# Delta rule: two sums of squares taken from rounded high and low parts, with the order tables set anew

## What is computed

```
q = l2_norm(q) * 128 ** -0.5 ; k = l2_norm(k)      # x * rsqrt(sum(x*x) + eps), sum over 128
kk = k k^T ; lower = strict(beta * kk * decay) ; sol = (I + lower)^-1 [v*beta, k*beta*exp(g)]
for each chunk:  v_new = u - w S ; o = q_dec S + qk v_new ; S = S*g_last + k_dec^T v_new
o = rms_norm(o, o_gain) * silu(z)                  # sum of o*o over 256
x = x + o @ w_out
```

## Time and profile before

| what | us |
|---|---|
| median of 3 runs | 1572.76 |
| the runs | 1573.16, 1568.33, 1572.76 |
| the profiled execution | 1573.43 |
| its span in the trace | 1571.5 |
| PE busy | 1538.3 (98%) |
| DVE busy | 897.3 (57%) |
| ACT busy | 751.1 (48%) |
| POOL busy | 258.9 (16%) |

### The profile page before, as it was taken

One profiled execution on the slowest core, in us unless ns is written; L12 is line 12 of the kernel. 1 busy time (PEld: TensorE's weight loads), 2 busy tenths in 40 slices (PEclk: granted clock), 3 DMA queues, 4 the chain that ended last, 5 costly groups with the idle time before them and its releaser, 6 DMA issues.

```text
span 1571.5 us, 20651 instructions
## 1 busy us (share of the span) xinstructions
PE 1538.3 (98%) x7640; PEld 1225.8 (78%) x7640; DVE 897.3 (57%) x1681; ACT 751.1 (48%) x1310; POOL 258.9 (16%) x453
## 2 busy tenths in 40 slices
PE   8989999999999999999999999999999999999998
PEld 6868888888888777777777787666678888888877
DVE  5667777776656366656667434555375243434476
ACT  4354455534543256666567323665555242322343
POOL 1033323433323003334333100000000000000000
PEclk9999999999989999999999999999999999999999
DMA  5221121111114232222222222121123322232221
GB/s 196 86 71 50 57 66 55 54 56 59 48 54 140 94 103 85 72 84 81 68 81 75 81 94 75 54 67 68 54 82 99 101 94 97 91 108 94 94 94 54
DMA packets 40163, 127.22 MB, mean 81 GB/s; under 512 B 4576, under 2 KB 9104, under 8 KB 40064
## 3 DMA queue, kind: packets, MB, share of 16 engines
q1 hardware_dynamic: 38112, 121.65, 24.0%
q0 software_dynamic: 1040, 3.27, 0.6%
q10 hardware_dynamic: 912, 0.99, 0.2%
HBM read 122.69 MB, written 2.15 MB: 79 GB/s over the span
## 4 chain that ended last, share of the span: by engine, by line
PE 87%; DVE 6%; ACT 3%; POOL 2%; issue 1%; DMA 0%; POOLq 0%; SPq 0%; ACTq 0%; DVEq 0%
PE ps L832 85%; PE ps L1194 2%; DVE wl L1941 1%; DVE qkv L1979 1%; PE ps L974 1%; ACT wh L1338 1%; ACT L L1747 1%; POOL L L2755 1%; DVE h L2589 1%; DVE mo L2583 1%; POOL uc L2725 1%; POOL masks L2723 0%; DVE L L2446 0%; DVE up L2076 0%; DVE cin L1993 0%
## 5 line engine op out<-in xcount | busy, mean ns | idle before, releaser
L832 PE MATMUL ps<-xr,wh 128*128 128x512 f32 x2752 | 882.8, 402 | 3.2 <-DVE xr L2382 1.2
L832 PEld LDWEIGHTS ps<-xr,wh 128*128 128x128 f32 x2752 | 507.0, 189 | 130.3 <-issue 31.0
L832 PE MATMUL ps<-xr,wl 128*128 128x512 f32 x1376 | 539.4, 392 | 0.0
L1941 DVE TENSOR_TENSOR wl<-wraw,wh 128x1024 fp32r<-128x1024 f32 x214 | 263.7, 1239 | 139.0 <-ACT wh L1338 137.4
L832 PEld LDWEIGHTS ps<-xr,wl 128*128 128x128 f32 x1376 | 259.4, 189 | 56.5
L1338 ACT ACTIVATE wh<-wraw 128x1024 fp32r<-128x1024 f32 x214 | 222.2, 1049 | 81.8 <-PE ps L832 79.9
L832 PE MATMUL ps<-xm,wh 128*128 128x512 f32 x640 | 198.8, 392 | 5.1 <-DVE xm L2576 2.7
L832 PEld LDWEIGHTS ps<-xm,wh 128*128 128x128 f32 x640 | 119.5, 188 | 33.6 <-DVE xm L2576 4.0
L2755 POOL TENSOR_SCALAR L<-L,m 128x256 f32<-128x256 f32 (+1 forms) x128 | 99.4, 796 | 272.0 <-DVE m L2461 272.0
L832 PE MATMUL ps<-xm,wl 128*128 128x512 f32 x320 | 124.6, 389 | 0.0
L1979 DVE SCALAR_TENSOR_TENSOR qkv<-cin,gains,qkv 128x512 f32<-128x512 f32 x96 | 81.8, 853 | 10.6 <-ACT qkv L1368 9.7
(11 more groups left out here) (265 smaller groups left out, 1754.6 us busy)
## 6 DMA issues: line engine op xcount, KB each, us to landing
wraw<-in_wa SPq DMA_DIRECT2D x48, 512.0 KB, 3.7
wraw<-in_wb SPq DMA_DIRECT2D x32, 512.0 KB, 4.2
wraw<-in_wu SPq DMA_DIRECT2D x32, 512.0 KB, 3.6
wraw<-in_wd SPq DMA_DIRECT2D x32, 512.0 KB, 3.7
wraw<-in_wao SPq DMA_DIRECT2D x16, 512.0 KB, 3.7
wraw<-in_wbo SPq DMA_DIRECT2D x16, 512.0 KB, 3.9
wraw<-in_wc SPq DMA_DIRECT2D x16, 512.0 KB, 3.7
bias<-rel_rows SPq DMA_DIRECT2D x16, 256.0 KB, 3.9
```

The costliest lines, as they stand in the source:

```text
L832: return e.matmul(out, w, x, start=start, stop=stop, skip_group_check=True)
L1941: e.tensor_tensor(m.wl[:, i % N_SPLIT, :], m.raw[:, i % N_RAW, :], m.wh[:, i % N_SPLIT, :].bitcast(F), ALU.subtract).then_inc(s.wlo, 1)
```

## The change

ACT makes a rounded copy of k's squares in `rqr[1]` (a new step "khi" in p1), DVE the rounded difference in `rqr[0]` ("klo", in p2), and PE sums both with a rounded matrix of ones, two fp32r products in place of one fp32 product. On PE the sum moves from p1 to p2 and waits for klo. For the output's squares DVE makes both parts (a copy and a difference, in r9), and PE's r10 waits for the second. The rounded ones are written by ACT once, in head 0's p1. The tables `a1`, `a2`, `a8`, `a9` and `a` are replaced.

```diff
-    "a1": plan("p1 p2 p2 p0 p2 p1 p1 p0 p1 p16 p14 p20 p10 p30"),
-    "a2": plan("p1 p4 p2 q0 p2 q4 q1 q2 q0 p0 q2 p0 q2 p0 q3 r0 p1 r0 r1 p0 r0 r2 r1 p0 r2 r0 r0 p4 r2 p0 p2 p0 r6"),
-    "a8": plan("p0 q1 p2 q3 q1 q0 p0 q0 p3 q0 p0 q0 p0 q0 p1 r1 r0 r1 r0 p0 r0 p2 p0 r0 p0 r0 p2 r5 p0 r1 p0 r2 r1"),
-    "a9": plan("q1 q5 q2 q5 q3 q1 q3 q2 r9 r1 r3 r0 r1 r0 r2 r0 r4 r2 r4"),
-    "a": plan("p0 q2 q0 p4 q2 q0 p1 p1 q4 q0 p0 q1 p0 q1 p0 r2 r2 r0 p1 r0 p3 p1 r0 p2 r0 r1 r2 r3 p1 r2 p0 p2 r16"),
+    "a1": plan("p5 p3 p1 p1 p0 p0 p0 p0 p4 p19 p16 p14 p34 p4"),
+    "a2": plan("p5 q2 p0 q2 q2 q0 p1 q0 p1 q0 p0 q1 p0 q0 p3 r1 p1 r0 p0 p3 p2 r1 p4 p5 r0 r1 r0 r0 r1 p0 r6 r3 r0"),
+    "a8": plan("q5 q2 p0 p0 q1 q1 p0 q0 p1 q2 q0 p0 q1 r0 p0 r0 p0 r1 p0 r0 p0 r0 r0 r1 p1 p2 r0 p3 p1 r0 p0 r0 r1"),
+    "a9": plan("q2 q6 q2 q7 q1 q2 q1 q4 r5 r2 r1 r0 r2 r0 r1 r2 r4 r2 r3"),
+    "a": plan("p1 q4 q3 p3 q2 q0 p0 q1 q0 p1 q0 p1 q0 p0 r2 p0 r6 p1 r2 r0 r0 p0 r2 r1 p0 p0 r0 p1 p4 r1 p4 r7 r5"),
...
+        yield
         cleared(PREP_BANK)
-        e.wait_ge(s.prep_a, prep_a(h, "sqk"))
-        end(mm(m.banks[PREP_BANK][:], m.ones, m.rq[:, 0, :]), (s.prep_a, prep_a(h, "lnk")))
-        yield
+        e.wait_ge(s.prep_v, prep_v(h, "klo"))
+        mm(m.banks[PREP_BANK][:], m.onesr[:], m.rqr[:, 1, :], True, False)
+        end(mm(m.banks[PREP_BANK][:], m.onesr[:], m.rqr[:, 0, :], False, True), (s.prep_a, prep_a(h, "lnk")))
         yield
...
-        e.wait_ge(s.rec_v, REC_V * h + 5)
-        mm(m.banks[5][:], m.ones, m.sqh[:, 0, :]).then_inc(s.rec_p, 1)
+        e.wait_ge(s.rec_v, REC_V * h + 7)
+        mm(m.banks[5][:], m.onesr[:], m.sqhr[:, 1, :], True, False)
+        mm(m.banks[5][:], m.onesr[:], m.sqhr[:, 0, :], False, True).then_inc(s.rec_p, 1)
...
+        else:
+            e.wait_ge(s.unit, 3)
+            e.activation(m.onesr[:], m.ones, ACT.Copy)
         did(e.activation(m.rq[:, 0, :], m.qkv[:, par, 1, :], ACT.Square))
+        after("sqk")
+        if h:
+            e.wait_ge(s.prep_v, prep_v(h - 1, "qdn"))
+        did(e.activation(m.rqr[:, 1, :], m.rq[:, 0, :], ACT.Copy))
...
-        yield from idle(3)
+        yield from idle(1)
+        e.wait_ge(s.prep_a, prep_a(h, "khi"))
+        did(e.tensor_tensor(m.rqr[:, 0, :], m.rq[:, 0, :], m.rqr[:, 1, :].bitcast(F), ALU.subtract))
+        yield from idle(2)
...
+        e.wait_ge(s.rec_v, REC_V * h + 5)
+        did(e.tensor_copy(m.sqhr[:, 1, :], m.sqh[:, 0, :]))
+        e.wait_ge(s.rec_v, REC_V * h + 6)
+        did(e.tensor_tensor(m.sqhr[:, 0, :], m.sqh[:, 0, :], m.sqhr[:, 1, :].bitcast(F), ALU.subtract))
```

More of the change, by code:

```diff
@@ L521, in __init__ @@
         self.k1 = top.new([6 * 128 + N_CC + 64], name="k1")
+        moff = top.p
         self.masks = top.new([7, 128], name="masks")
+        self.onesr = at(moff + 512, [128], R, "ones")
         self.gains = top.new([N_GAIN + 128], name="gains")
@@ L549, in __init__ @@
         self.nb = a.new([15, 64], name="nb")
+        soff = a.p
         self.sqh = a.new([2, 512], name="sqh")
+        roff = a.p
         self.rq = a.new([2, 512], name="rq")
+        self.sqhr, self.rqr = at(soff, [2, 512], R, "sqhr"), at(roff, [2, 512], R, "rqr")
         self.qd = a.new([2, 512], name="qd")
@@ L746 @@
 PREP_A = {n: i + 1 for i, n in enumerate(
-    ("silu1", "sqk", "silu0", "silu2", "silu3", "lnk", "exk", "eb", "E", "sqq", "v0", "v1"))}
-PREP_V = {n: i + 1 for i, n in enumerate(("dv", "y", "at", "qk", "kg", "kd", "dc", "qdn", "U3", "T3"))}
+    ("silu1", "sqk", "khi", "silu0", "silu2", "silu3", "lnk", "exk", "eb", "E", "sqq", "v0", "v1"))}
+PREP_V = {n: i + 1 for i, n in enumerate(("klo", "dv", "y", "at", "qk", "kg", "kd", "dc", "qdn", "U3", "T3"))}
 PREP_O = {n: i + 1 for i, n in enumerate(("sel", "D"))}
@@ L754 @@
 LEV_O = {n: i + 1 for i, n in enumerate(("M4", "M5", "M6"))}
-REC_P, REC_A, REC_V = 12, 8, 9
+REC_P, REC_A, REC_V = 12, 8, 11
 STICK_P = {n: i + 1 for i, n in enumerate(
@@ L1089, in recur @@
         for j in range(2):
-            clear[6 + j] = [(s.rec_a, REC_A * h + 5 + j), (s.rec_v, REC_V * h + 6 + j)]
+            clear[6 + j] = [(s.rec_a, REC_A * h + 5 + j), (s.rec_v, REC_V * h + 8 + j)]
         yield
         cleared(5)
-        e.wait_ge(s.rec_v, REC_V * h + 5)
-        mm(m.banks[5][:], m.ones, m.sqh[:, 0, :]).then_inc(s.rec_p, 1)
+        e.wait_ge(s.rec_v, REC_V * h + 7)
+        mm(m.banks[5][:], m.onesr[:], m.sqhr[:, 1, :], True, False)
+        mm(m.banks[5][:], m.onesr[:], m.sqhr[:, 0, :], False, True).then_inc(s.rec_p, 1)
         clear[5] = [(s.rec_a, REC_A * h + 7)]
@@ L1608, in split_o @@
             e.wait_ge(s.wused, BLOCK["wa", 6 * HEADS - 1] + 1)
-        e.wait_ge(s.rec_v, REC_V * (i // 2) + 8 + i % 2)
+        e.wait_ge(s.rec_v, REC_V * (i // 2) + 10 + i % 2)
         e.activation(m.XR[:, i, :], m.XF[:, 16 + i, :], ACT.Copy).then_inc(s.ohi, 1)
@@ L2336, in recur @@
             e.wait_ge(s.rec_a, REC_A * h + 8)
-            e.wait_ge(s.rec_v, REC_V * h + 6 + j)
+            e.wait_ge(s.rec_v, REC_V * h + 8 + j)
             did(e.tensor_tensor(o, o, m.sqh[:, 0, :], ALU.mult))
```

## The result

| what | before | after |
|---|---|---|
| median, us | 1571.15 (4 runs) | 1578.54 (4 runs) |
| the profiled execution | 1573.43 | 1578.58 |
| its span | 1571.5 | 1576.5 |

The ratio is 1.0046, with a 95% interval of 1.0034 to 1.0059: slower, by 7.4 us in the medians and 5.0 us in the two spans. The forecast was 1573.3 and "no change". The time lies inside the range, on the side that I had given 0.24.

The account below looks back on a forecast made before the run. PE was taken as the bound, busy for 1538.3 of 1571.5 us. The terms -6.6 + 0.3 + 5.1 + 1.0 + 1.9 - 1.7 + 0.5 gave +0.5 us, so 1573.3 against the median 1572.76; range 1565.5 to 1579.5.

Parts of the forecast that it names:

- The price of a sum: On PE, two fp32r products take 0.45 us against 0.86; each sum saves 0.41 us, sixteen save 6.6 us.
- D: Rival: the sums save nothing, an fp32r pair taking as long as one fp32 product; +7.1 us, 1579.9, chance 0.02.
- P4 of head 0: At the start, P4 of head 0 starts 2.35 us later, at 117.0, with some 7 us idle before it.
- P4(0) to stage 3: Behind the start: 2.7 us of work left for later, and +1.0 us for the low clock behind P4 of head 0.
- The work left undone: Before P4 of head 0, fewer triples and no ks and G of head 1 are issued, leaving 2.7 us for later.
- The clock: At the start, half clock again when P4 of head 0 starts: +1.0 us, bounds no change and +3.4.
- Stages 3 to 7: Table a: PE reaches ks about when klo ends; +0.3 us for all stages, bounds 0 and 2.5.
- C: Rival: klo comes late in every stage of table a, behind a split of weights; +6.2 us, 1579.0, chance 0.20.
- The turn: Stage 8 to stage 9: longer wait for Tm, later shuffles and slower POOL steps; +1.9 us.
- The clock at the turn: The slow 10.2 us stretch at stage 8 to 9 shortens halfway towards 3.4: -1.7 us, bounds -5.1 and 0.
- stage 9: Its own output sum waits for a longer chain on ACT and DVE; +0.5 us, bounds 0 and 1.9.
- A: The forecast itself: start and turn give the gain back; +0.5 us, own range 1568.5 to 1577.5, chance 0.56.

Follow-up runs that it names:

- first_ks_old: The changed kernel with stage 1 as before: ks of head 0 is one fp32 product at the head, klo(0) not computed, old table a1; 1577.28 us, ratio 1.0029.
- tables_old_sums: The kernel before with the new tables alone: both sums stay single fp32 products, no added DVE or ACT work; 1584.26 us, ratio 1.0078.
- mid_split2: The changed kernel with one gemm step of table a moved between v1 and B2, taken from the four behind p13; 1576.40 us, ratio 1.0028.
- out_sum_only: The kernel before, its tables kept, with the output's sum alone taken from rounded parts; 1575.75 us, ratio 1.0032.
- early_klo: The changed kernel edited to take klo(0) at p1 on DVE, with ks(0) behind one gemm step instead of five; 1582.55 us, ratio 1.0069.
- fill_six: The changed kernel with six gemm steps of stage 2 moved ahead of P4 of head 0; 1582.27 us, ratio 1.0064.
- out_sum_late: out_sum_only with one gemm step (tables a, a8) or two (a2, a9) moved from behind ones to ahead of it; 1578.06 us, ratio 1.0048.
- fill_klo1: fill_six with klo of head 1 moved on DVE to the head of stage 2; 1579.12 us, ratio 1.0048.

## Why the prediction was right or wrong

**The price of a sum: right.** 0.45 us predicted, 0.46 measured (219.12 to 219.58), and 0.83 us per middle stage for two. D is out.

**P4 of head 0: right in kind, short in size.** Forecast 2.35 us later, measured 2.94 (tables alone 2.5, the rest klo's 0.76 us of idle). The idle time before it was 4.55 us, not 7, and 9.5 instead of 11 in all: PE ran the triples ahead of it at half clock from 102.3 to 105.7, which used up 1.7 us of it. The work left undone, 2.7 us, was right; first_ks_old shows the cause.

**P4(0) to stage 3: the term that failed most.** It takes 5.43 us more. Of that 2.7 was forecast as work left over, and -0.4 belongs to ones(0). The clock took 1.7, since it was low from 115.7 to 122.6, 6.8 us instead of 3.4; I had taken 1.0. Two more waits stand in it, 0.30 and 0.47 us. The rest of some 0.7 us leaves no idle time on record; about 0.5 of it is what two waits cost beyond theirs (0.24 us each, see the last section). And 0.8 us of the error is a double count in my sum. The -6.6 held all sixteen sums, but ks(0) was in the chain to P4(0) with its new length already, and ks(1) in the work left over with its new price.

**Stages 3 to 7: the second failed term.** The forecast was -4.1 + 0.3; measured -1.16. klo was in time (at 219.12 without a wait), so C is out, though its sign was right. What I had not priced at all is the order of the small products. I had checked each new wait and taken the rest of a table as free; tables_old_sums gives it as 0.50 us per stage, 2.5 in five, with 0.5 more at the first of them (U4 of head 1, 0.31 us idle and 0.24 beyond that).

**The turn: right in kind, and in size by two errors that cancel.** Stage 8 to P4(7) is +1.25, where the terms made +1.1. The first shuffle stands 0.74 us later in its stage than before (429.89 - 406.32 against 423.70 - 400.87), where I had 0.3. POOL's chain for head 7 took 13.23 us instead of 12.73, where I had 0.8. ones(6) waited 1.00 us and P4(7) 0.65, less than my 2 to 3 because the wait at ones had taken its place. The two of POOL's steps that stand beside DVE's added copy and difference took 0.38 and 0.58 us, where they had taken 0.22:

```profile
440.62 0.43 DVE L2346 CAST sqhr<-sqh 128x512 fp32r<-128x512 f32 x1
441.09 0.69 DVE L2348 TENSOR_TENSOR sqhr<-sqh,sqhr 128x512 fp32r<-128x512 f32 x1
```
```profile
440.75 0.38 POOL L2747 TENSOR_TENSOR uc<-uc,masks 128x16 f32<-128x16 f32 x1
441.27 0.58 POOL L2745 TENSOR_TENSOR masks<-nb,uc 128x12 f32<-128x12 f32 x1
```

That is 0.5 us for 1.12 us of DVE work. Each of the two steps starts 0.13 or 0.18 us into a DVE operation and ends 0.07 to 0.08 us after that operation's end, so it pays only for what was left of it. The Trainium skill (SBUF — State Buffer, "SBUF: two separate sides") calls the shared port pair an exclusive lock for a whole instruction. The trace agrees with it; the full length of the added operations, 1.1 us, was not paid.

**The clock at the turn and stage 9.** The slow stretch shrank from 10.2 to 3.4 us, -3.4 where I had -1.7. The new a9 took it back: without their slow stretches P4(7) to ones(7) is 34.1 us before (39.17 - 5.1) and 35.8 after (37.48 - 1.7), and 35.95 was measured in mid_split2, which has none. No wait stood at ones(7), for which I had put 0.5. The sum of the rest, -1.70, is what the terms gave (-1.7 + 0.5 - 0.4); that two errors of 1.7 cancel in it was luck.

**The sum.** Forecast +0.5; spans +5.0, or +6.8 with the start of stage 1 left out. The difference, by the stretches of the table 6.2, is made of 3.5 at the start (2.94 + 5.43 against 2.35 + 2.7 - 1.2 + 1.0), 2.6 in stages 3 to 7 and 0.1 elsewhere.

**The range.** By my own yardstick of 0.3% the kernel is slower, and not "no change": 1578.54 lies above 1577.5, the upper edge of A's own range. It lies inside the stated range only because I had drawn that up to C's price, and C's mechanism didn't occur. That is luck.

## What to carry to other kernels

Price a new order by itself, with the old operations in it; here the order cost more than the operations saved. When a sum is replaced by a cheaper one with a longer chain ahead of it, ask first which engine's queue its result sits in and who is behind it, and only then how much PE it saves. Before filling idle time with work from elsewhere, list what that work issues on the other queues: if one of them is the reason for the idle time, the work will come out behind it.

## What the runs showed of the hardware

A wait of PE costs more than its idle time on record, here by 0.24 us each time. Where a sum of two fp32r products waits behind a triple at full clock, its start is 0.15 to 0.17 us later than the idle time says, and 0.07 to 0.09 us more pass to the next start: 0.24 us together, the same for 0.29 us of idle time (ks(7) in after), 0.33 (out_sum_only), 0.76 (ks(0) in after) and 3.47 (early_klo). For a short wait this nearly doubles the cost. Three places of about 0.3 us of idle time cost some 0.55 each.

A slowed step of POOL ends just after the DVE operation beside it: 0.07 and 0.08 us after it at 440.75 and 441.27 in after, 0.10 at 432.05 in before, 0.13 at 105.76 in early_klo.

The idle time at the start was often paid twice, because a stretch at 1.2 GHz began in or just behind it: at 102 and at 115 us in after (3.4 and 6.8 us long), at 102 and at 123 in fill_six, at 156 behind the 2.49 us of out_sum_late. It isn't so each time: out_sum_only has the tables of before there and the same 1.77 us of idle time before P4(0), and no low stretch, where before has 3.4 us. After's stretch at 102 us cost nothing on the path to P4(0), since idle time followed it. The low stretch at the turn is 10.2 us long in before and in out_sum_only, and 13.7 in out_sum_late, all with old tables; with the new ones it is 3.4 in after, and it is missing in fill_klo1 and in mid_split2, whose turn has the same table and the same waits as after's (0.65, 0.56, 0.56 against 0.65, 0.56, 0.57). What decides stays open. Executions of one kernel differ too: of the eleven of before that ran beside tables_old_sums, the fastest, 1567.73 us, has a granted clock of 0.997, and the one at the median, 1571.61, has 0.993. So a low stretch that one profile shows isn't shown to belong to its kernel.
